# A third pair of half-depth products and shares spread through memory, in a one-core decoder step

## What is computed

```python
z = x @ w_in                                     # 1024 prompt rows, 8 sample rows
q, k, v, qi, ki, wi, u, vb, ga, gb = jnp.split(z, offsets, axis=-1)
dots = jnp.einsum('bthd,bsd->bths', qi, ki)      # indexer: 4 heads of 64
score = jnp.einsum('bths,bth->bts', jax.nn.relu(dots), wi) * scale
# 256 best visible keys of each query, then, with 8 heads of 64:
logits = jnp.einsum('bthd,btkhd->bthk', q, ks) * HEAD_DIM ** -0.5
p = jax.nn.softmax(jnp.where(valid, logits, NEG_INF), axis=-1)
out = jnp.einsum('bthk,btkhd->bthd', p, vs)
```

## Time and profile before

| what | value |
|---|---|
| timed runs | 1365.23 us median of 3 (1361.83 to 1366.84) |
| the profiled execution's own time | 1355.75 us |
| its span, first to last instruction | 1354.3 us |
| TensorE busy | 1304.8 us, 96% of the span |
| VectorE busy | 760.6 us, 56% |
| ScalarE busy | 309.3 us, 23% |
| TensorE clock granted, mean | 0.993 of full |

### The profile page before, as it was taken

How to read it: one execution, slowest core, us unless ns; L and a number is a source line. 1 busy time by engine, 2 the same in 40 slices (tenths; PEclk the granted TensorE clock), 3 DMA queues, 4 the chain that set the end, 5 groups by cost and what they waited for, 6 DMA issues and landing times. The chain is left out here.

```text
span 1354.3 us, 19345 instructions
## 1 busy us (share of the span) xinstructions
PE 1304.8 (96%) x6621; PEld 667.5 (49%) x6621; DVE 760.6 (56%) x1826; ACT 309.3 (23%) x696; POOL 243.5 (18%) x292
## 2 busy tenths in 40 slices
PE   8999999899999999999999989999999999999984
PEld 2444444345466666666577656544443333333321
DVE  2332223599899889998278844566663232332135
ACT  0100112322321111111266630011122222222224
POOL 3231000043330000010133500011121111111112
PEclk9999999999999999999999999999999999999997
DMA  9412002210032221110234319831138999999936
GB/s 324 111 38 63 34 17 79 90 57 0 0 112 70 71 70 70 70 69 23 61 104 152 96 42 363 343 142 32 32 118 332 390 392 408 408 407 410 378 154 252
DMA packets 71486, 216.26 MB, mean 160 GB/s; under 512 B 16195, under 2 KB 42051, under 8 KB 61034
## 3 DMA queue, kind: packets, MB, share of 16 engines
q1 hardware_dynamic: 53978, 182.63, 35.9%
q0 software_dynamic: 12688, 27.76, 6.0%
q10 hardware_dynamic: 4736, 4.75, 1.1%
HBM read 188.57 MB, written 34.66 MB: 165 GB/s over the span
## 5 line engine op out<-in xcount | busy, mean ns | idle before, releaser
L1146 DVE TENSOR_SCALAR_CACHE_REDUCE front<-score_all,bound 128x384 bf16<-128x384 f32 (+2 forms) x198 | 174.0, 940 | 0.4 <-DVE bound L1168 0.3
L313 PE MATMUL ps<-front,x_all 128*128 128x512 f32 (+1 forms) x320 | 124.1, 542 | 0.8 <-ACT z L500 0.8
L1872 PE MATMUL ps<-w_o,mergedT 128*128 128x512 f32 x256 | 116.5, 601 | 0.0
L2314 PE MATMUL ps<-w_gate_up,w_o 128*32 128x512 f32 (+1 forms) x640 | 113.2, 594 | 1.5 <-DVE w_o L2403 1.5
L966 PE MATMUL ps<-x_all,front 128*128 128x344 f32 x384 | 114.4, 453 | 0.0
L966 PE MATMUL ps<-x_all,w_gate 128*128 128x344 f32 x384 | 113.3, 453 | 0.0
L2314 PE MATMUL ps<-w_a,w_o 128*64 128x512 f32 (+1 forms) x256 | 113.1, 594 | 0.0
L966 PEld LDWEIGHTS ps<-x_all,w_gate 128*128 128x128 f32 x384 | 72.7, 190 | 37.5
L2430 DVE TENSOR_TENSOR w_o<-w_o,ps 128x256 f32<-128x256 f32 x24 | 10.1, 421 | 144.1 <-ACT w_o L2382 144.1
L966 PEld LDWEIGHTS ps<-x_all,front 128*128 128x128 f32 x384 | 72.6, 190 | 37.1
L313 PEld LDWEIGHTS ps<-front,x_all 128*128 128x128 f32 x320 | 59.4, 190 | 59.1 <-issue 48.3
(11 more groups left out here) (381 smaller groups left out, 2019.6 us busy)
## 6 DMA issues: line engine op xcount, KB each, us to landing
w_gate_up<-in_w_gate_up SPq DMA_DIRECT2D x16, 2048.0 KB, 13.5
w_down<-in_w_down SPq DMA_DIRECT2D x16, 1024.0 KB, 14.7
w_a<-in_w_gate_up SPq DMA_DIRECT2D x8, 2048.0 KB, 11.0
mergedT<-in_w_gate_up SPq DMA_DIRECT2D x8, 2048.0 KB, 16.4
gates<-in_w_down SPq DMA_DIRECT2D x8, 1024.0 KB, 6.6
mergedT<-in_w_down SPq DMA_DIRECT2D x8, 1024.0 KB, 8.9
front<-in_w_qkvi SPq DMA_DIRECT2D x7, 930.0 KB, 15.8
w_gate<-in_w_gate SPq DMA_DIRECT2D x4, 1280.0 KB, 6.3
```

The lines of the kernel that those rows point to most:

```text
L313: mm = nc.tensor.matmul(ps[:, n % 2, 0:c1 - c0], x_all[:, k, t * P:(t + 1) * P], w[:, k, c0:c1], start=(k == 0), stop=(k == KC - 1))
L1146: V.tensor_scalar(waste[0:n, at - width:at], s, column(bound, g), None, compare, ALU.add, accum_out=column(number, g)).then_inc(taken, 1)
L1872: mm = nc.tensor.matmul(ps[:, PROJECTED[i % 2][c], :], mergedT[:, k, t * P:(t + 1) * P], w_o[:, k, c * 512:(c + 1) * 512], start=(k == 0), ...
L2314: mm = nc.tensor.matmul(ps[c0:c1, GU, :], rowsT[j][:, k, c0:c1], w_gu[b][:, k, :], start=(k == 0), stop=(k == KC - 1))
```

## The change

1. Tiles 5 and 6 become a third pair; only tile 7 is made plainly. The restoring of t3 moves along. The score units begin in tile 6 and follow each other more closely, some in the middle of a make. The two accumulator banks change places (`bank_of`), so the first make waits for the other of tile 0's reads.
2. For the first pair, VectorE's row sums and t3 are moved behind the copies of turned rows.
3. For tiles 7 to 3 (the five wide ones) `spread_shares` is gone. SP stores the inverted totals into memory, head by head, and loads them back into both halves of the partitions; ScalarE copies OUT to attnT as it is; VectorE multiplies attnT in place with the shares one tile later (`share_far`). Tiles 2 to 0 stay as they were.
4. The semaphores of the last big stage are cleared only inside the conditional block.

```diff
-        FIRST_SINGLE = 5
+        FIRST_SINGLE = 7
+        def bank_of(n):
+            return (n + 1) % 2
             def wait_for_bank(n):
-                pe.wait_ge(acc_read, act_reads(n - 2) if n >= 2 else AFTER_FEW + 1 + n)
+                pe.wait_ge(acc_read, act_reads(n - 2) if n >= 2 else AFTER_FEW + 2 - n)
...
                 for k in range(KC):
+                    if k == HALF and unit is not None:
+                        score_dots(unit)
...
             make_pair(3)
+            make_pair(5)
+            t = NT - 1
             pe.wait_ge(weight_sums, 3 * HALF + 2)
-            for t in range(FIRST_SINGLE, NT):
...
+            make(t, 0, slot(t, 0), unit=3)
+            turn(t - 1)
+            score_dots(4)
+            make(t, 1, slot(t, 1), unit=5)
+            score_dots(6)
+            make(t, 2, slot(t, 2))
+            score_dots(7)
+            make(t, 3, slot(t, 3), unit=8)
+            score_dots(9)
...
-            sum_rows(1)
-            dve.wait_ge(acc_full, 1 + 4)
-            nc.vector.tensor_tensor(t3, wk[:, HALF:KC], t3, ALU.subtract).then_inc(weight_sums, 1)
             for a in range(1, FIRST_SINGLE, 2):
                 if a == 1:
                     read_few_turned()
                 read_turned(a - 1)
                 if a == 1:
+                    sum_rows(a)
+                    dve.wait_ge(acc_full, 1 + 4)
+                    nc.vector.tensor_tensor(t3, wk[:, HALF:KC], t3, ALU.subtract).then_inc(weight_sums, 1)
...
+            def spread_far_shares(at):
+                t = order[at]
+                sp.wait_ge(inverted, at + 1)
+                sp.dma_start(scratch["far_shares"][t].rearrange("h q -> q h"), total[t % 2][:], allow_slow_non_contiguous=True).then_inc(shares_out, 16)
+                sp.wait_ge(shares_out, 16 * (at + 1))
+                if at >= 1:
+                    sp.wait_ge(far_shared, at)
+                for e in range(2):
+                    sp.dma_start(by_pair(shares)[e * HD:(e + 1) * HD],
+                                 scratch["far_shares"][t:t + 1].rearrange("o (k e) q -> o e k q", e=2)[:, e].to_broadcast([HD, PAIRS, P])
+                                 ).then_inc(far_shares_in, 16)
...
-                    if units[s - 2][1] == PAIRS - 1:
+                    if units[s - 2][1] == PAIRS - 1 and order.index(units[s - 2][0]) >= N_FAR:
                         spread_shares(units[s - 2][0])
...
+                            before = order.index(t) - 1
+                            if before <= N_FAR:
+                                act.wait_ge(shares_out, 16 * before)
...
+                    if at < N_FAR:
+                        act.wait_ge(weighted, (at + 1) * PAIRS)
+                        t = order[at]
+                        nc.scalar.copy(attnT[:, :, t * P:(t + 1) * P], by_pair(ps[:, OUT, :])).then_inc(out_read, 1)
...
+            def share_far(at):
+                mine = attnT[:, :, order[at] * P:(order[at] + 1) * P]
+                dve.wait_ge(far_shares_in, 32 * (at + 1))
+                dve.wait_ge(out_read, at + 1)
+                nc.vector.tensor_tensor(mine, mine, by_pair(shares), ALU.mult).then_inc(far_shared, 1)
...
+        spent_semaphores = ExitStack()
+        spent_semaphores.enter_context(nc.cleanup_on_exit())
         merge_route_and_experts(nc, ins, outs, keep, scratch)
...
         with nc.If(longest > SHARE):
+            spent_semaphores.close()
```

More of the change, by code:

```diff
@@ L339, in make_pair @@
                     turn_wi()
+                if a == 5:
+                    for c in (4, 1, 2, 3):
+                        few_score(c)
                 pe.wait_ge(weight_sums, 3 * HALF)
@@ L357, in make_pair @@
                 make(a + 1, 2, slot(a + 1, "qi_b"))
-                make(a + 1, 3, slot(a + 1, "v_b"))
+                if a == 5:
+                    score_dots(0)
+                make(a + 1, 3, slot(a + 1, "v_b"), unit=1 if a == 5 else None)
                 turn(a)
+                if a == 5:
+                    score_dots(2)
             def turn_few():
@@ L451, in _ @@
             make_pair(3)
+            make_pair(5)
+            t = NT - 1
             pe.wait_ge(weight_sums, 3 * HALF + 2)
-            for t in range(FIRST_SINGLE, NT):
[L454 to L466, removed]
+            pe.wait_ge(x_in[t], 16)
+            make(t, 0, slot(t, 0), unit=3)
[7 more added lines that the diff above has]
+            score_dots(9)
             make_few_uv(range(0, KC // 2))
@@ L548, in _ @@
             read_pair(3)
[L549 to L559, removed]
+            read_pair(5)
+            t = NT - 1
+            wait_for_rows(t)
+            rectify(3)
+            read(t, 0, slot(t, 0))
+            rectify(4)
+            rectify(5)
+            read(t, 1, slot(t, 1))
+            rectify(6)
+            read(t, 2, slot(t, 2))
+            rectify(7)
+            rectify(8)
+            read(t, 3, slot(t, 3))
+            rectify(9)
             for n in range(len(units) - 2, len(units)):
@@ L1317, in _, with load_query @@
             sp.dma_start(own_b[:], ins["rank"][:, 0:N_SAMPLE]).then_inc(own_in, 16)
-            for b in range(N_SAMPLE):
+            def load_query(b):
                 if b >= Q_AHEAD:
@@ L1500, in _ @@
                         if hp == 0 and e == 0 and s >= 2 * PAIRS:
-                            act.wait_ge(spread, order.index(t) - 1)
+                            before = order.index(t) - 1
+                            if before <= N_FAR:
+                                act.wait_ge(shares_out, 16 * before)
+                            else:
+                                act.wait_ge(spread, before - N_FAR)
                         row = probs[s % 2][:, e, 0:(t + 1) * P]
@@ L1613, in _ @@
                 if s >= 2 and units[s - 2][1] == PAIRS - 1:
-                    share_out(units[s - 2][0])
+                    at = order.index(units[s - 2][0])
+                    if 1 <= at <= N_FAR:
+                        share_far(at - 1)
+                    if at >= N_FAR:
+                        share_out(units[s - 2][0])
 N_EXPERTS = 32
```

103 lines of the change are left out of this document (67 added, 36 removed).

## The result

The changed kernel took 1368.04 us (median of 21 runs, 1362.79 to 1377.68) beside 1362.82 us for the kernel before on the same chip (21 runs, 1360.14 to 1368.09): a ratio of 1.0036, 95% interval 1.0023 to 1.0049. It is 0.36% or 5 us slower where 0.75% (10.3 us) faster was forecast, outside the range of 1349 to 1362.

What follows compares the result with a forecast made beforehand. TensorE's matmuls (busy 96%) were taken as the limit almost everywhere, VectorE right behind in one attention stretch. Terms -3.4 - 1.4 - 4.3 - 1.2 = -10.3 us took the median 1365.23 to 1354.9 us; range 1349 to 1362.

Steps and rivals of the forecast that it cites:

- the way through memory: Attention, shares of five tiles: store (5.1 us) and loads, about 9 us together, hidden behind the next tile; 0, bound +3.
- The slower rival: Store in small pieces takes 21 us or more, holding up VectorE's masking in five tiles; at 25 us, 1394 us; chance 0.06.
- Third pair: Projection, tiles 5 and 6: 28 matmuls instead of 32, VectorE's added work costing TensorE no wait; -3.4 us.
- VectorE's order: Projection's start: turned rows copied first, -1.9 us, against +0.5 for the exchange of banks; together -1.4, bounds 0 and -2.2.
- Packed score units: Projection, tiles 6 and 7: four matmuls (3.43 us) between score units cover ScalarE's rectifications; 0, bound 3 us.
- The end: Kernel's end: clearing the semaphores and the barrier behind it leave the path; -1.2 us.
- Shares off TensorE: Attention, five tiles: 8 matmuls (0.98 us) per tile leave TensorE; -4.3 us, bounds -2 and -5.5.
- the stretch with VectorE full: Attention stretch beginning at 755.73, VectorE busy 12.20 of 12.85 us: only 0.35 of the 0.98 us can be had.
- full in all five stretches: Attention, from one spread of shares to the next: TensorE is full in all five stretches, so its matmuls are the limit.

Runs made afterwards that it cites:

- the pair above: Second profile of the unchanged changed kernel (1364.54 us) beside the profile of the changed kernel with each store written flat; attention 12.1 us longer than the latter's 140.1.
- the table: Eight kernels, the changed one and variants storing 4-byte pieces at other spacings, only one head's, or flat: landings 10.9 to 2.3 us, ratios 1.0036 to 0.9923.
- e5_turned: Changed kernel with the five tiles' totals turned by a TensorE transpose and ScalarE copy before the store: 1352.22 us, ratio to the kernel before 0.9910.
- e1_proj: Kernel before with only the projection part (third pair, scores behind it, VectorE's order, banks): 1356.74 us beside 1363.20, ratio 0.9951.
- e13_rest5: Changed kernel with the attention of before, so projection and cleanup parts only, in more rounds: 1358.67 us beside 1364.18 of the kernel before, ratio 0.9959.
- e12_turned5: Changed kernel with totals turned by TensorE before the store, again in more rounds: 1354.53 us beside 1364.18 of the kernel before, ratio 0.9923.
- the flat store: Changed kernel with each far_shares store written as 32 contiguous bytes per partition, shares landing in another order: 1353.15 us, ratio to the kernel before 0.9939.

## Why the prediction failed

*The step that failed* is the way through memory, "I take 0, bound +3". It was wrong twice. The store was priced at 5.1 us, 64 pieces of 50 ns on each engine behind 1.9, from a queue whose packets have nothing to do with these; it took 10.9, and the error isn't the price of a piece: the same 1024 pieces spaced widely landed in 3.4 to 4.0 us together with a flat store, under my estimate. And I asked only who waits for the store, when the cost is what others lose while it is under way. Even 10.9 us made nobody wait for the store but ScalarE, by 0.66 us at tile 3, the place that I had named as tight. The cost was 13 us all the same: idle time of TensorE (5.9 us in the pair above) and lower granted clock (at most 6.2). Of the idle time, 2 to 3 us are a wait for gathers that the change doesn't touch; what the other waits were for is open, and the late instruction fetches are only suspected. The base was off too, by less: the median of three that I subtracted from, 1365.23, is 2.4 us above that of 21.

*The slower rival* had the right object and the wrong mechanism. It needed a landing of 21 us and a full hold-up of VectorE; landings were 9 to 12 us (16 and 17 behind w_a), VectorE stood 1.4 us in all before its five products of shares, and for ScalarE, not for the loads, and the kernel was slower all the same. At 0.07 for slower and 0.20 for within 0.5%, this outcome, inside the 0.5% on the slow side, had too little.

The Trainium skill (DMA: Bandwidth & Descriptors, Specifications) says that transfers below 512 bytes are done as read-modify-write. By that rule alone all layouts of the table would suffer alike, and the trace doesn't agree: 3.4 against 10.9 us. With the addition that such writes wait for each other where they fall close together, it would give the table's order; no run shows that mechanism. The Trainium skill's advice (DMA: Bandwidth & Descriptors, Rules for kernel authors) to make the last dimension contiguous agrees with e5_turned, 1.2 us to land.

*The other terms held.* Third pair and VectorE's order: 4.8 forecast, 5.0 at the next stage's first matmul, 6.7 (4.6 to 8.6) by the ratio of e1_proj. Packed score units: 0, and 0. The end: 1.2 and 1.2. Shares off TensorE: 4.3 forecast, 4.1 between e13_rest5 and e12_turned5, and 144.9 - 140.1 = 4.8 in two profiles of attention with equally little half clock (3.4 us). The reason was in part another. The busy time fell by 130.41 - 126.18 = 4.2 us for the five spreads, near the 4.9 that they last. Of the stretch with VectorE full I had taken only 0.35 us; that stretch was one of the quick first profile, and in the second one TensorE waits at 762.45 for VectorE's product of shares, a wait that the change removes (others of about its length came instead: idle time fell by 0.6 us only). The sum of all without the store's cost, -10.3, is what the kernels with a harmless store measured: 10.9 and 9.7 us by the medians for the turned totals, 10.1 for the flat store.

## What to carry to other kernels

- Before a DMA writes 4-byte pieces, look at how close together they land in memory. Here pieces 16 bytes or more apart were harmless; sixteen in 64 bytes took three times as long to land, and in that kernel the gathers took half as long again and the instruction fetches three times as long. If the data must be dense, turn it first: a TensorE transpose of 128x8 and one small copy cost less than could be measured.
- Price a transfer twice: by who waits for it, and by what else uses the memory while it is under way. The second is never on the chain of waits of the kernel before.
- When the profiled execution lies 7 us under the median, its waits may not be the usual ones; "full in all five stretches" held in one of two profiles.
- A releaser named in a row of waits can be wrong: look whether the transfer was issued in this stage at all (one was 490 us old here).

## What the runs showed of the hardware

- Landing of dense 4-byte stores: 9.4 to 11.8 us for 1024 pieces in the changed kernel's two profiles where nothing stood ahead, 8.0 for 128, 16.4 for the first two in a row; with eight in 64 bytes 4.9 to 6.6, with four or one 3.4 to 4.0 (these and the 128 with a flat store behind them). The queue's own row hardly shows it (q1 14.8% against 11.8%): the time is in q0's row, 31.5% against 21.1%. Beside a dense store in flight the gathers move 68 packets in 10 us, behind it 276 in 4.
- Between runs of one kernel the granted clock goes with the spread: the six runs of e12_turned5 go from 1348.98 us at 0.994 to 1357.59 at 0.988, 1.4 us for each 0.001. It isn't so everywhere: the changed kernel has 1368.04 us at 0.987 and 1373.23 at 0.988.
- Open: whether the instruction fetches that came late are what the stalls without a right releaser were waiting for. The slow ones lie beside the stores (3.1, 2.0 and 1.4 us on q14 at 714, 743 and 746 us of the changed kernel, 0.3 to 0.7 with the flat store), but no run separates them from the gathers.
